# Modulation pairs in a hybrid transformer trunk: VectorE's additions moved ahead of softmax, rotation and normalisation steps, a pair's products put behind each sweep's first scores

## The reference

```python
cond = silu(c)                                   # one vector for context, one for latent tokens
m = split(cond @ w_ada[l] + b_ada[l], 6)         # w_ada[l]: 1024 x 6144
h = x * (1 + m[1]) + m[0]
x = layer_norm(ALPHA * x + (1 + m[2]) * mixer(h), ln_mix_g[l], ln_mix_b[l])
h = x * (1 + m[4]) + m[3]
x = layer_norm(ALPHA * x + (1 + m[5]) * moe(h), ln_ffn_g[l], ln_ffn_b[l])
```

## Time and profile before

| | us |
|---|---|
| median of 3 runs | 2241.32 |
| lowest, highest | 2234.8, 2241.38 |
| the profiled execution's own time | 2243.87 |
| its span | 2242.1 |
| mean granted TensorE clock | 0.957 of full speed |

### The profile page before, as it was taken

How to read it: one execution, slowest core, us unless ns; L and a number is a source line. 1 busy time by engine, 2 the same in 40 slices (tenths; PEclk the granted TensorE clock), 3 DMA queues, 4 the chain that set the end, 5 groups by cost and what they waited for, 6 DMA issues and landing times.

```text
span 2242.1 us, 44959 instructions
## 1 busy us (share of the span) xinstructions
PE 2037.6 (91%) x18880; PEld 1426.6 (64%) x18881; DVE 1337.0 (60%) x2625; ACT 1034.7 (46%) x1783; POOL 245.3 (11%) x363
## 2 busy tenths in 40 slices
PE   5999999898998898799889988999899999988996
PEld 3566666657775575587756655777556666556774
DVE  2566665437896242489831324789656666537896
ACT  3344344226774241476622322776534444316774
POOL 0432222100001000100010001000122223200000
PEclk8999999799999999899999998999999999998998
DMA  9244343245895335388733353688412111124880
GB/s 374 93 146 153 119 162 132 103 150 206 284 321 209 137 134 186 114 301 301 273 136 123 141 188 132 243 292 309 141 52 68 63 44 68 44 78 154 283 315 29
DMA packets 56768, 381.22 MB, mean 170 GB/s; under 512 B 6384, under 2 KB 10480, under 8 KB 12000
## 3 DMA queue, kind: packets, MB, share of 16 engines
q1 hardware_dynamic: 51552, 373.00, 46.8%
q10 hardware_dynamic: 4608, 4.20, 0.5%
q0 software_dynamic: 384, 0.89, 0.1%
HBM read 373.96 MB, written 4.10 MB: 169 GB/s over the span
## 4 chain that ended last, share of the span: by engine, by line
PE 76%; DVE 14%; ACT 4%; issue 4%; DMA 1%; SPq 0%; ACTq 0%; DVEq 0%
PE ps L834 15%; PE ps L1486 6%; DVE e_wlo L2795 6%; PE ps L1490 5%; PE ps L1489 5%; PE ps L742 4%; PE ps L786 4%; PE ps L762 4%; PE ps L974 3%; PE ps L1271 3%; DVE bufx L2813 2%; PE ps L797 2%; PE ps L1442 2%; ACT e_whi L1666 2%; PE ps L1373 2%
## 5 line engine op out<-in xcount | busy, mean ns | idle before, releaser
L2795 DVE TENSOR_TENSOR e_wlo<-ring,e_whi 128x1024 fp32r<-128x1024 f32 x384 | 456.1, 1221 | 91.6 <-ACT e_whi L1666 76.0
L1666 ACT ACTIVATE e_whi<-ring 128x1024 fp32r<-128x1024 f32 x384 | 402.9, 1060 | 118.9 <-PE ps L1490 115.7
L834 PE MATMUL ps<-bufh,ring 128*128 128x384 f32 x1024 | 394.7, 507 | 6.7 <-ACT bufo L1722 4.7
L834 PEld LDWEIGHTS ps<-bufh,ring 128*128 128x128 f32 x1024 | 177.5, 192 | 98.8 <-issue 24.1
L1486 PE MATMUL ps<-e_whi,e_hs 128*128 128x512 f32 x512 | 210.5, 411 | 28.7 <-DVE e_wlo L2795 25.5
L1666 ACT ACTIVATE scratch<-ps 128x384 f32<-128x384 f32 (+6 forms) x311 | 109.1, 368 | 231.4 <-PE ps L834 53.7
L1490 PE MATMUL ps<-e_whi,e_hs 128*128 128x512 f32 x512 | 200.4, 391 | 0.0
L1489 PE MATMUL ps<-e_wlo,e_hs 128*128 128x512 f32 x512 | 199.8, 390 | 0.0
L742 PE MATMUL ps<-ring,silc 128*32 128x128 f32 x3072 | 116.6, 311 | 53.7 <-DVE mod L2188 32.6
L2923 POOL TENSOR_SCALAR bufx<-bufo,x_gb 128x384 f32<-128x384 f32 x56 | 37.0, 675 | 1111.0 <-DVE bufo L2234 1111.0
L742 PEld LDWEIGHTS ps<-ring,silc 128*32 128x32 f32 x3072 | 97.6, 125 | 68.9 <-issue 50.7
(11 more groups left out here) (312 smaller groups left out, 3508.0 us busy)
## 6 DMA issues: line engine op xcount, KB each, us to landing
ring<-in_moe SPq DMA_DIRECT2D x192, 1024.0 KB, 4.9
ring<-in_w_ada SPq DMA_DIRECT2D x96, 1024.0 KB, 5.7
ring<-in_gdn_w_in SPq DMA_DIRECT2D x32, 1024.0 KB, 6.8
ring<-in_gdn_w_out SPq DMA_DIRECT2D x8, 1024.0 KB, 4.8
ring<-in_gqa_w_in SPq DMA_DIRECT2D x6, 1024.0 KB, 4.9
ring<-in_gqa_w_out SPq DMA_DIRECT2D x4, 1024.0 KB, 6.3
ring<-in_mla_w_out SPq DMA_DIRECT2D x4, 1024.0 KB, 7.4
ring<-in_mla_w_in SPq DMA_DIRECT2D x3, 1024.0 KB, 4.9
```

Source lines behind the costliest of these rows:

```text
L834: last = mm(ps[:, head_bank(n, m), 0:T], w[:, m % 2, kt, :], bufh[:, kt, :], start=(kt == 0), stop=(kt == KT - 1))
L1666: return op(out, in_, ACT.Copy, **kw)
L2795: return tt_(e_wlo[:, b, :], w, e_whi[:, b, :].bitcast(F32), ALU.subtract)
```

## The change

Four edits. In a layer norm, VectorE's addition of pair 0 goes from behind the fourth normalisation to ahead of the wait for `dev_ready`. Before a sweep, VectorE's addition of pair 0 goes ahead of the first head pair's rotation and reciprocal (GQA) or ahead of the reciprocal and the rotation (MLA). TensorE's products of pair 1 go from before the last piece of preparation to behind the first scores of the sweep; VectorE's addition of pair 1 stays behind `weights(0)`. In the sweep, the addition in turn n goes ahead of `weights(n + 1)`.

```diff
@@ sweep, TensorE
                 score(0)
+                ada_pair("mixer", l, 1)
                 for n in range(H * TT):
@@ gqa, TensorE
                 ada_pair("mixer", l, 0)
                 gqa_pair_ready(0)
-                ada_pair("mixer", l, 1)
                 gqa_proj(l, *GQA_PIECES[-1])
@@ layer_norm, VectorE
                     tt_(tiles, tiles, spread(ps[:, 6, 0:T], 2), ALU.subtract).then_inc(centred, 1)
+                if stage:
+                    stage_add(*stage, 0)
                 dve.wait_ge(dev_ready, n + 1)
...
                     tt_(bufo[:, k, :], rbuf[:, k, :], ps[:, 6, 0:T], ALU.mult).then_inc(normed, 1)
-                    if stage and k == 3:
-                        stage_add(*stage, 0)
@@ sweep, VectorE
                 for n in range(H * TT):
+                    if n in SWEEP_TURNS:
+                        stage_add("mixer", l, SWEEP_TURNS[n])
                     if n + 1 < H * TT:
                         weights(n + 1)
-                    if n in SWEEP_TURNS:
-                        stage_add("mixer", l, SWEEP_TURNS[n])
                     joint(n)
@@ gqa, VectorE
+                stage_add("mixer", l, 0)
                 gqa_pair_ready(0)
-                stage_add("mixer", l, 0)
```

## The result

| | before | after |
|---|---|---|
| median (lowest to highest), us | 2241.35 (2234.8 to 2253.06), 4 runs | 2209.99 (2208.72 to 2218.14), 4 runs |
| profiled execution, us | 2243.87 | 2209.7 |
| span, us | 2242.1 | 2207.9 |
| mean granted clock | 0.957 | 0.964 |

The ratio of the times is 0.9852, with a 95% interval from 0.9818 to 0.9886. The changed kernel is 1.5% faster, 31.4 us by the medians and 34.2 us by the two traces. The forecast was 2210 us.

What follows compares the result with a forecast made beforehand. TensorE, 76% of the chain, was taken to bound the kernel, idling 32.6 us for VectorE's additions. Norms 11.1, GQA start 6.3, MLA start 1.4, last turns 7.4 and 8.0 sum to 34.2 us off 2243.87: 2210 us, range 2201 to 2220.

Steps and rivals of the forecast that it cites:

- start of GQA: Before the GQA sweep: first scores 6.1 us earlier, plus a little for work at half clock; 6.3 us (5.5 to 7.5).
- start of MLA: Before the MLA sweep: no wait goes, but pair 1 leaves the path to the first scores; 1.4 us (0.8 to 2.0).
- last turns of MLA, turn 18 included: End of the MLA sweep: TensorE is the longer side, turn 23 at 1316.8 against 1325.80; 8.0 us (6 to 9).
- The wait of 32.6 us: TensorE's largest wait: a pair's first matmul waited for VectorE's addition 13 times; called neither floor nor ceiling of the gain.
- 0.68: Layer norms: normalisation of the upper four tiles and VectorE's three modulated tiles come 0.68 us earlier.
- 0.9 each: Mid norms, before the router: its matmuls end closer behind the modulated tiles; 2.7 us for three (2.0 to 3.3).
- the first rival: Norms give only VectorE's share, 0.68 us each, 4.1 in all, and the rest its lower ends; 2222 us, chance 0.12.
- my best and worst cases: Tail norms of layers 0 and 1: gain 5.4 us at best, 1.8 if the clock stays at 1.2 GHz; 3.5 taken.
- pair 1 fits into the first softmax: GQA start: pair 1 (2 us) and second scores (0.8) end at 766.7, within the 3.53 us softmax ending at 766.9.
- The walk's total: GQA's last turns, reckoned turn by turn: turn 23 at 856.85 against 864.77, gain 7.9; 7.4 us taken (5.5 to 8).
- The two rivals on the clock: Whole kernel: clock gives more, 2201 us, chance 0.12; or low stretches after norms make it slower, 2250 us, chance 0.03.
- the one that has the clock give more: Whole kernel: TensorE idles less, 1.2 GHz stretches after the waits vanish, all upper ends; 2201 us, chance 0.12.

Runs made afterwards that it cites:

- norm_products_held: Changed kernel with TensorE's pair 1 in every norm held until the fourth tile is normalised; 2209.66 us in one run.
- shadow: Changed kernel with the sweep's addition moved inside the next softmax, between scaled maximum and wait for the exponentials; 2209.5 us, ratio to before 0.9860.
- start_products: Kernel before with only TensorE's pair 1 moved behind the sweep's first scores, VectorE's additions unmoved; 2242.87 us in one run.
- additions_doubled: Changed kernel with each moved addition, and that of pair 1 before a sweep, done twice; 2200.51 us in one run.
- norms_only: Kernel before with only VectorE's addition of pair 0 in norms moved ahead of the wait for dev_ready; 2232.18 us against 2244.6, ratio 0.9969.
- norm_units_split: Changed kernel with the first unit of pair 1 in each norm moved behind the variance matmuls; 2212.75 us, ratio to before 0.9850.

## Why the prediction was right

The terms of the sum against what their stretches lost:

| term | predicted | measured |
|---|---|---|
| mid norms, three | 2.7 | 1.9 (0.50 + 0.86 + 0.52) |
| tail norms of layers 0 and 1 | 7.0 | 6.9 (3.61 + 3.28) |
| tail norm of layer 2 | 1.4 | 1.2 |
| start of GQA | 6.3 | 6.0 (9.57 - 3.61) |
| start of MLA | 1.4 | 1.7 (5.02 - 3.28) |
| last turns of GQA, turn 18 included | 7.4 | 7.8 (2.28 + 5.55) |
| last turns of MLA, turn 18 included | 8.0 | 8.9 (1.30 + 7.62) |
| sum | 34.2 | 34.4 |

The spans differ by 34.2 us. Outside these stretches GQA's second turn gained 1.6 us (72.84 - 68.93, less 2.28), since it had run at 1.2 GHz before, and the rest (experts, DeltaNet, output projections) lost 1.8 on balance. That forecast and result agree to within 1 us is luck: single terms are off by up to 0.9, these two cancel, and runs of one kernel differ by 9 to 26 us. What the traces bear out is the size of each term.

- *The view.* The wait of 32.6 us was the right entry to follow, but not the size of the gain, and that the sum of 34.4 lies close to it is chance. The norms' waits of 17.2 us gave 10.0, the 2.69 at the start of GQA gave 6.0, the start of MLA gave 1.7 with no wait at all, and the 12.7 in the last turns gave 16.7.
- *Norms.* The addition's new place was covered. The last modulated tile came 0.55 us earlier in tail norm 0 (7.09 to 6.54 behind the broadcast), not 0.68, because the three tiles took 2.71 us instead of 2.59; why they did is not shown. In the mid norms I counted 0.9 each; they gave 0.6 on average, since the last tile came only 0.50 us earlier there (in layer 1, 908.61 - 902.08 against 927.43 - 920.40), and norm_products_held shows it to be VectorE's share alone. That is the first rival, right for four of the six norms and wrong for the two that mattered. In the tail norms the clock stood between my best and worst cases: pair 1 still ran at 1.2 GHz in both, the tile did not. My best case, a gain of 5.4, was too good: at the full clock all through (shadow) a tail norm takes 8.15 us, a gain of 4.4 in layer 0.
- *Starts.* The step "pair 1 fits into the first softmax" held to 0.3 us. The step that went with it, VectorE's earlier addition, was counted at nothing lost; it is also nothing gained once the products have moved (start_products).
- *Turns.* The walk's total held, two of its steps did not. I had softmax and addition in series as the pace of turn 20, 2.9 us, and turns of 2.4 for softmax alone; measured are 2.69, 2.58, 2.90, 2.64 and 2.57. The errors cancelled. additions_doubled shows that most of the addition lies in VectorE's wait for scores there: half a microsecond more made turn 20 only 0.16 longer.
- *The clock.* Of MLA's 8.9 us some 1.7 are less time at the low clock: with the old order but the norms' edit the same turns took 22.01 us instead of 23.72. The two rivals on the clock did not come in this trace: it has 159 us at 1.2 GHz instead of 193, and of the 34 us between them some 16 lie in the two sweeps and 10 between the tail norms and the sweeps. But the one that has the clock give more was nearer than its chance of 0.12 suggests: with the same norms, shadow and additions_doubled had some 132 us, and additions_doubled took 2200.51, that rival's 2201. By the Trainium skill's rule that activity releases the throttle (TensorE: Matmul & The Clock Gate, "What's actually happening") less idle time in the norms should leave less time at the low clock. The traces agree in direction. In the five kernels with the old order in the norms, at least 3.4 us of the 12 us behind each of 30 broadcasts were at 1.2 GHz, 6.5 on average; in the four with the new order and no split (the changed kernel, norms_only, additions_doubled, shadow) it was 3.4 at most in 24, 1.3 on average, and nothing in 13.
- *Exclusion of VectorE and GpSimd.* The 0.25 us of a long addition did go, and the trace agrees with the Trainium skill (SBUF — State Buffer, "SBUF: two separate sides"): 168 ns at most, against 416.

## What to carry to other kernels

A product that nobody wants yet still stops the matmul engine if it shares its one bank with the product before it; look at what the other engine has in its queue ahead of emptying that bank, not at how long emptying takes. Put the emptying where the other engine waits for the matmul engine's next result, and put the filler product where the matmul engine waits for a chain of the others (the first softmax of a sweep); then the timeline tells in advance about how much of each move will be covered. Where runs differ by more than the part in question, compare the same stretch in two traces rather than two times.

## What the runs showed of the hardware

Pair 1 right behind the broadcast ran at 1.2 GHz in one execution and at 2.4 in another of nearly the same kernel (3.62 us in the changed kernel, 1.95 in norms_only, tail norm of layer 0), after the same work. What did change with the edit is how much of it there was: behind a norm's broadcast, with TensorE idle for 2.9 us before pair 1, at least 3.4 us of the next 12 us were at 1.2 GHz in each of 30 cases; with pair 1 right behind the broadcast it was 0 to 3.4 us in 24 cases. An addition of VectorE that took 166 to 168 ns alone took 407 to 416 beside GpSimd's operation on 128x384 elements, six times out of six. Stretches of unchanged code moved by as much as 8 us between executions: from the tail norm of layer 2 through the DeltaNet to the next norm 406.9 us in shadow with 10.2 us at 1.2 GHz in it, 407.5 before with 17.1, 408.2 in the changed kernel with 13.7, and 415.4 in norm_units_split with 34.1.
